# Feed-forward up projections with the weight tiles stationary and the transposed tokens moving

## The reference

```
def squared_relu_mlp(x, w_up, w_down):          # first block, hidden width 4096
    return jnp.square(jax.nn.relu(x @ w_up)) @ w_down

def swiglu(h, w_in, w_out):                     # second block, twice, hidden width 2816
    a, b = jnp.split(h @ w_in, 2, axis=-1)
    return (jax.nn.silu(a) * b) @ w_out
```

## Time and profile before

| | us |
|---|---|
| median of 3 runs | 1234.88 (1234.44, 1234.88, 1235.19) |
| span of the profiled execution, first to last instruction | 1232.4 |
| PE busy | 1114.9 (90%) |
| PE weight loads | 922.5 (75%) |
| DVE busy | 843.9 (68%) |
| ACT busy | 502.0 (41%) |
| stage M, up(0) to the start of its last down | about 152 to 337 |
| stage F2A | about 595 to 787 |
| stage F2B | about 1036 to 1220 |

### The profile page before, as it was taken

How to read it: one execution, slowest core, us unless ns; L and a number is a source line. 1 busy time by engine, 2 the same in 40 slices (tenths; PEclk the granted TensorE clock), 3 DMA queues, 4 the chain that set the end, 5 groups by cost and what they waited for, 6 DMA issues and landing times.

```text
span 1232.4 us, 15193 instructions
## 1 busy us (share of the span) xinstructions
PE 1114.9 (90%) x5509; PEld 922.5 (75%) x5509; DVE 843.9 (68%) x1145; ACT 502.0 (41%) x679; POOL 77.4 (6%) x79
## 2 busy tenths in 40 slices
PE   4999699999969988769999999789969998999997
PEld 3887578888758877767788888589756776788885
DVE  5777566677567778986587778688666876445543
ACT  6335354544434754312434343234244433343441
POOL 1000100000010005530000000000200000000000
PEclk9999899999989999979899999879879999999999
DMA  9961459678367750013398798657212002665541
GB/s 321 353 230 63 154 218 325 241 259 293 128 243 259 276 180 1 1 69 103 134 330 286 283 318 272 221 199 222 69 69 69 2 12 91 205 204 189 169 152 68
DMA packets 125604, 224.28 MB, mean 182 GB/s; under 512 B 4760, under 2 KB 58232, under 8 KB 125432
## 3 DMA queue, kind: packets, MB, share of 16 engines
q1 hardware_dynamic: 124904, 221.02, 51.6%
q0 software_dynamic: 656, 2.69, 0.7%
HBM read 222.64 MB, written 1.05 MB: 182 GB/s over the span
## 4 chain that ended last, share of the span: by engine, by line
PE 49%; DVE 4%; ACT 1%; issue 1%; POOL 0%; POOLq 0%; ACTq 0%; DVEq 0%
PE psum L1365 46%; PE psum L1799 1%; PE psum L1655 1%; DVE arena L927 1%; DVE res L964 0%; DVE arena L963 0%; PE psum L1394 0%; PE psum L1382 0%; DVE xlo L934 0%; ACT arena L822 0%; POOL arena L506 0%; ACT arena L581 0%; DVE arena L913 0%; PE psum L1734 0%; ACT arena L842 0%
## 5 line engine op out<-in xcount | busy, mean ns | idle before, releaser
L872 DVE TENSOR_TENSOR wlo<-raw,whi 128x2048 fp32r<-128x2048 f32 (+2 forms) x172 | 340.3, 1992 | 207.1 <-ACT whi L576 206.8
L576 ACT CAST whi<-raw 128x2048 fp32r<-128x2048 f32 (+2 forms) x172 | 287.2, 1675 | 218.6 <-PE psum L1365 215.8
L1365 PE MATMUL psum<-whi,xhi 128*128 128x512 f32 (+1 forms) x896 | 355.0, 396 | 18.1 <-DVE xlo L934 10.9
L1365 PE MATMUL psum<-whi,xlo 128*128 128x512 f32 (+1 forms) x896 | 350.2, 391 | 0.0
L1365 PE MATMUL psum<-wlo,xhi 128*128 128x512 f32 (+1 forms) x896 | 350.0, 391 | 0.0
L1365 PEld LDWEIGHTS psum<-whi,xhi 128*128 128x128 f32 x896 | 171.7, 192 | 53.5 <-issue 21.5
L1365 PEld LDWEIGHTS psum<-whi,xlo 128*128 128x128 f32 x896 | 171.1, 191 | 34.1
L1365 PEld LDWEIGHTS psum<-wlo,xhi 128*128 128x128 f32 x896 | 171.8, 192 | 32.2
L890 DVE SCALAR_TENSOR_TENSOR adaacc<-adaw,cact,adaacc 128x512 f32<-128x512 f32 x196 | 147.3, 751 | 6.4
L1365 PE MATMUL psum<-whi,hhi 128*128 128x512 f32 x304 | 120.2, 395 | 5.6 <-DVE hlo L1151 2.8
L1365 PE MATMUL psum<-wlo,hhi 128*128 128x512 f32 x304 | 119.0, 391 | 0.0
(11 more groups left out here) (227 smaller groups left out, 1091.3 us busy)
## 6 DMA issues: line engine op xcount, KB each, us to landing
adaw<-in_ada_w SPq DMA_DIRECT2D x48, 1024.0 KB, 5.7
raw<-in_ffn_w_in SPq DMA_DIRECT2D x88, 512.0 KB
raw<-in_ffn_w_out SPq DMA_DIRECT2D x44, 512.0 KB
raw<-in_w_up SPq DMA_DIRECT2D x16, 1024.0 KB
raw<-in_w_down SPq DMA_DIRECT2D x16, 1024.0 KB
raw<-in_hgrn_w_in SPq DMA_DIRECT2D x16, 1024.0 KB
raw<-in_attn_w_qkv SPq DMA_DIRECT2D x12, 1024.0 KB
adaw<-in_kv_ada_w SPq DMA_DIRECT2D x8, 1024.0 KB, 5.2
```

The costliest lines, as they stand in the source:

```text
L576: sc.copy(whi[:, s, 0:width], raw[:, s, 0:width]).then_inc(hi_ready[s], 1)
L872: ve.tensor_tensor(wlo[:, s, 0:width], raw[:, s, 0:width], whi[:, s, 0:width].bitcast(F32), ALU.subtract).then_inc(lo_ready[s], 1)
L1365: return te.matmul(dst, lhsT, rhs, start=start, stop=stop, skip_group_check=open_)
```

## The change

In `up` the roles of the operands are exchanged. The stationary operand is a 128x128 tile of the weights, the moving one all 256 tokens of a depth tile. Four hidden tiles `f` stand in the place of the two token tiles; two of them share a bank. The result comes out with the hidden dimension on the partitions, and the transposes and the semaphore `h_turned` go. In M, ACT's relu now works on 2x256 values of a bank, and its square reads `relu` in SBUF instead of the transposed PSUM. In F2A and F2B one silu over bank 4 and one product with bank 5 replace two of each, and the cast and subtraction read `gat` in SBUF. New waits: PE waits for `act_done` (M) or `gate_done` (F2A, F2B) ahead of the next `up`, ACT for `used[3]` (the down before) ahead of the cast into `hhi`, and ACT (M) and DVE (F2A, F2B) for `h_lo` ahead of writing `sq` and `gat`.

```
             def up(n, fresh=None):
...
-                    for i in range(TT):
+                    for f in range(4):
+                        dst = psum[:, 4 + f // 2, (f % 2) * T:(f % 2 + 1) * T]
                         for k in range(4):
-                            kt = 4 * s + k
-                            ins = three(psum[:, 4 + i, :], xhi[:, kt, i * P:(i + 1) * P], xlo[:, kt, i * P:(i + 1) * P],
-                                        s, k * 512, 512, kt == 0, kt == KD - 1)
+                            kt, c = 4 * s + k, k * 512 + f * P
+                            mm(dst, whi[:, s, c:c + P], xhi[:, kt, :], kt == 0 and f % 2 == 0, False, True)
+                            mm(dst, whi[:, s, c:c + P], xlo[:, kt, :], False, False, True)
+                            ins = mm(dst, wlo[:, s, c:c + P], xhi[:, kt, :], False, kt == KD - 1, True)
                     ins.then_inc(used[s], 1)
...
             up(Q_FF1, fresh=1)
-            hidden1(0)
             with pe.Fori(1, N_FF1) as t:
+                pe.wait_ge(act_done, 2 * t)
                 up(t + Q_FF1)
                 pe.wait_ge(h_lo, 2 * t)
                 down(t + (Q_FF1 - 1), 2, slots=(2,))
+                pe.wait_ge(ada_saved, t + (A_FF1 - 1))
                 ada(t + (A_FF1 - 1))
                 down(t + (Q_FF1 - 1), 2, slots=(3,))
-                hidden1(t)
...
                 up(q0, fresh)
-                mlp2_hidden(0, gb)
                 with pe.Fori(1, N_FF2) as t:
+                    pe.wait_ge(gate_done, t + gb)
                     up(t + q0)
                     pe.wait_ge(h_lo, t + hb)
                     down(t + (q0 - 1), 1)
...
-                    mlp2_hidden(t, gb)
```

ACT in M, ACT in F2A and F2B, and DVE in F2A and F2B:

```
-                for i in range(TT):
-                    sc.activation(relu[:, i, :], psum[:, 4 + i, :], ACT.Relu).then_inc(act_done, 1)
+                for b in range(2):
+                    sc.activation(relu[:, 2 * b:2 * b + 2, :], psum[:, 4 + b, :].rearrange("p (k t) -> p k t", k=2),
+                                  ACT.Relu).then_inc(act_done, 1)
...
                 for b in range(2):
-                    act.wait_ge(h_turned, 2 * t + b + 1)
-                    sc.activation(sq[:, 2 * b:2 * b + 2, :], psum[:, 6 + b, :].rearrange("p (k t) -> p k t", k=2),
-                                  ACT.Square).then_inc(h_sq, 1)
+                    act.wait_ge(act_done, 2 * t + b + 1)
+                    if not first:
+                        act.wait_ge(h_lo, 2 * t)
+                    sc.activation(sq[:, 2 * b:2 * b + 2, :], relu[:, 2 * b:2 * b + 2, :], ACT.Square).then_inc(h_sq, 1)
                     act.wait_ge(h_sq, 2 * t + b + 1)
+                    if not first:
+                        act.wait_ge(used[3], t + Q_FF1)
                     sc.copy(hhi[:, 2 * b:2 * b + 2, :], sq[:, 2 * b:2 * b + 2, :]).then_inc(h_hi, 1)
...
-                for i in range(TT):
-                    sc.activation(sil[:, i, :], psum[:, 4 + i, 0:256], ACT.Silu).then_inc(act_done, 1)
+                sc.activation(sil, psum[:, 4, :].rearrange("p (k t) -> p k t", k=2), ACT.Silu).then_inc(act_done, 1)
...
-                act.wait_ge(h_turned, t + (hb + 1))
-                sc.copy(hhi[:, 0:2, :], psum[:, 6, :].rearrange("p (k t) -> p k t", k=2)).then_inc(h_hi, 1)
+                act.wait_ge(gate_done, t + (gb + 1))
+                if not first:
+                    act.wait_ge(used[3], t + q0)
+                sc.copy(hhi[:, 0:2, :], gat).then_inc(h_hi, 1)
...
-                for i in range(TT):
-                    v.wait_ge(act_done, 2 * t + (gb + 16 + i + 1))
-                    ve.tensor_tensor(gat[:, i, :], sil[:, i, :], psum[:, 4 + i, 256:512], ALU.mult).then_inc(gate_done, 1)
+                v.wait_ge(act_done, t + (gb + 2 * N_FF1 + 1))
+                if not first:
+                    v.wait_ge(h_lo, t + hb)
+                ve.tensor_tensor(gat, sil, psum[:, 5, :].rearrange("p (k t) -> p k t", k=2), ALU.mult).then_inc(gate_done, 1)
...
-                ve.tensor_tensor(hlo[:, 0:2, :], psum[:, 6, :].rearrange("p (k t) -> p k t", k=2),
-                                 hhi[:, 0:2, :].bitcast(F32), ALU.subtract).then_inc(h_lo, 1)
+                ve.tensor_tensor(hlo[:, 0:2, :], gat, hhi[:, 0:2, :].bitcast(F32), ALU.subtract).then_inc(h_lo, 1)
```

More of the change, by code:

```diff
@@ L215, in build @@
         st1 = area(11520, 2, 8)
-        relu = area(0, TT, 512)
+        relu = area(0, 4, T)
         sq = area(1024, 4, T)
-        sil = area(2048, TT, T)
-        gat = area(2560, TT, T)
+        sil = area(2048, 2, T)
+        gat = area(2560, 2, T)
         hin = area(0, 4, TT, D)
@@ L286, in build @@
         acc_done = sem("acc_done")
-        act_done, gate_done, h_turned, h_sq, h_hi, h_lo = [sem(s) for s in ("act_done", "gate_done", "h_turned", "h_sq", "h_hi", "h_lo")]
+        act_done, gate_done, h_sq, h_hi, h_lo = [sem(s) for s in ("act_done", "gate_done", "h_sq", "h_hi", "h_lo")]
         bg_turned, bg_saved = sem("bg_turned"), sem("bg_saved")
@@ L763, in _, with mlp2 @@
             split(3, Q_F2A, 1024)
-            def mlp2(t, q0, hb, first=False, nxt=2048, last=False):
+            def mlp2(t, q0, hb, gb, first=False, nxt=2048, last=False):
                 if not last:
@@ L774, in mlp2 @@
                     split(2, t + q0, 1024)
-                act.wait_ge(h_turned, t + (hb + 1))
-                sc.copy(hhi[:, 0:2, :], psum[:, 6, :].rearrange("p (k t) -> p k t", k=2)).then_inc(h_hi, 1)
+                act.wait_ge(gate_done, t + (gb + 1))
+                if not first:
+                    act.wait_ge(used[3], t + q0)
+                sc.copy(hhi[:, 0:2, :], gat).then_inc(h_hi, 1)
                 if not first:
                     split(3, t + q0, 1024)
-            mlp2(0, Q_F2A, HT_F2A, first=True)
+            mlp2(0, Q_F2A, HT_F2A, 0, first=True)
             with act.Fori(1, N_FF2 - 1) as t:
-                mlp2(t, Q_F2A, HT_F2A)
-            mlp2(N_FF2 - 1, Q_F2A, HT_F2A, nxt=1536)
+                mlp2(t, Q_F2A, HT_F2A, 0)
+            mlp2(N_FF2 - 1, Q_F2A, HT_F2A, 0, nxt=1536)
             split(2, Q_KV, 1536)
@@ L857, in _ @@
             split(3, Q_F2B, 1024)
-            mlp2(0, Q_F2B, HT_F2B, first=True)
+            mlp2(0, Q_F2B, HT_F2B, N_FF2, first=True)
             with act.Fori(1, N_FF2 - 1) as t:
-                mlp2(t, Q_F2B, HT_F2B)
-            mlp2(N_FF2 - 1, Q_F2B, HT_F2B, last=True)
+                mlp2(t, Q_F2B, HT_F2B, N_FF2)
+            mlp2(N_FF2 - 1, Q_F2B, HT_F2B, N_FF2, last=True)
         @block.vector
@@ L1352, in _ @@
             split(3, Q_F2B, 1024)
-            mlp2(0, Q_F2B, HT_F2B, 2 * N_FF2, first=True)
+            mlp2(0, Q_F2B, HT_F2B, N_FF2, first=True)
             with v.Fori(1, N_FF2 - 1) as t:
-                mlp2(t, Q_F2B, HT_F2B, 2 * N_FF2)
-            mlp2(N_FF2 - 1, Q_F2B, HT_F2B, 2 * N_FF2, last=True)
+                mlp2(t, Q_F2B, HT_F2B, N_FF2)
+            mlp2(N_FF2 - 1, Q_F2B, HT_F2B, N_FF2, last=True)
             residual(5)
@@ L1648, in _ @@
             norm(3, gates=2)
[L1650 to L1656, removed]
             def mlp2(q0, hb, gb, fresh, m0=None):
@@ L1818, in _ @@
             norm(5, gates=4)
-            mlp2(Q_F2B, HT_F2B, 2 * N_FF2, 6)
+            mlp2(Q_F2B, HT_F2B, N_FF2, 6)
 _INS = ["x", "norm_mix_pre", "norm_mix_post", "norm_ffn_pre", "norm_ffn_post", "w_up", "w_down", "attn_w_qkv", "attn_w_o",
```

## The result

The changed kernel takes 1236.98 us (median of 15 runs, 1235.82 to 1238.62) where the kernel before takes 1234.85 us (15 runs, 1232.38 to 1235.53) on the same chip. The ratio is 1.0023, 95% interval 1.0015 to 1.0030: 2 to 4 us slower, at the edge of the 2.5 us that I had called no change. I forecast 1235.3 with a range of 1215 to 1251, and 0.39, 0.38 and 0.23 for same, slower and faster.

What follows compares the result with a forecast made beforehand. PE's matmul stream was taken to bound the kernel. Narrow matmuls added 18.4 us and removed transposes, restarts and waits saved about 18.3, so +0.4 with a remaining restart: 1235.3 us, range 1215 to 1251.

Steps and rivals of the forecast that it cites:

- The price of a matmul by its width: In `up`, a matmul of 256 columns costs 0.1200 us, columns plus surcharge; over 30 items this adds 18.4 us.
- 0.1249: Rival pitch in `up`, us a matmul: load and surcharge one after the other, 1249.4 us; chance 0.27 for anything above 0.1209.
- 0.1134: Rival pitch in `up`, us a matmul: the surcharge halves as at 128 columns, 1216.3 us; chance 0.17 for anything below 0.1191.
- 0.1118: Lowest pitch in `up` by the trace, us a matmul: the load's floor, 1211.7 us; within the 0.17 for below 0.1191.
- 0.109: Pitch in `up` by the Trainium skill's back-to-back rule, us a matmul: about 1204 us; chance 0.02 of the 0.17.
- Transposes and restart: PE time removed per item: 0.87 us in M (7 items, -6.1), 0.46 in F2B (ten items, -4.6) and in F2A.
- The wait at the side product in F2A: PE's wait of 0.21 us for DVE ahead of the side product's matmuls disappears, in 9 items.
- The ends: Ahead of the last `down`: M saves 1.05 us (wait 2.75), F2B 0.45 (1.55 instead of 2.00), F2A counted as nothing.
- F2B as a whole: Stage F2B: narrow matmuls added, then -4.6 for transposes and restart, +0.15 at the first item, -0.45 at the end.
- The clock: Side rival: stretches of half clock, 1.75 us for one after F2A's last wait, vanish or appear, -2 to +4 us; chance 0.10.
- The sum: Whole kernel: all terms give +0.05 us, +0.4 with the restart behind F2A's side product, so the saving is paid back.
- From the span to the time: Whole kernel: runs lie 2.5 us above the profiled span, so a span of 1232.8 becomes a time of 1235.3 us.

Runs made afterwards that it cites:

- M only: Exchange of operands and missing transposes in the first feed-forward layer (M) only, F2A and F2B as in the kernel before: 1234.06 us against 1234.24, ratio 1.0000.
- few transposes: The kernel before with 1 of every 4 transposes kept, matmuls and waits otherwise as before: 1223.50 us against 1234.24, ratio 0.9920.
- F2A and F2B only: The change in F2A and F2B only, M as in the kernel before: 1236.36 us against 1234.24, ratio 1.0020.
- the early start: M's last `down` starts slot 2 after the first half of the hidden values: changed kernel 1233.36 us, M only 1230.17, kernel before 1234.74.

## Why the prediction was right, and where it was off

- *The price of a matmul by its width:* right. 0.1200 was taken, 0.1199 measured; the other pitches that I weighed (0.1249, 0.1134, 0.1118, 0.109) fell. The term it carries, +18.4 us for 30 items, stands: 30 x (11.51-10.91) = 18.0.
- *Transposes and restart:* right. By the periods, an item of M gained 0.25 (0.26 forecast), one of F2A 0.05 (0.06), one of F2B lost 0.19 (0.15, taken from a period 0.03 longer than the others).
- *The wait at the side product in F2A:* right, it went.
- *The ends:* M's last `down` starts 3.06 us after the start of the matmul ahead, 2.83 after the stream, where I had 2.75; the one of F2B 1.65 after the stream, where I had 1.55. Small shortfalls. At F2A's end, where I took nothing, the last `down` starts 8.08 us after the one before it, instead of 8.28.
- *F2B as a whole:* was to lose 1.8 (6.7-4.6+0.15-0.45) and lost 2.26. Most of the difference is the period, nine times 0.04 us, and the rest the end. I also left the restart behind the first wait out of the new order, though PE's first two matmuls there are 0.2 apart as after any wait. That is about 0.1 us, but it doesn't show in the sum: the stretch from F2B's start to its first `down` grew by 0.86 us (25.44 to 26.30), where my terms give 0.9.
- *The clock:* it made most of the distance between forecast and result. I had priced a stretch of half clock at 1.75 us and named F2A's end for it; it kept its place there. In the profiled execution a new one came at M's last `down`, 1.62 us, and M's start had 0.94 us more of it, while F2A's start had about 0.6 less than before. I had given the clock as a side rival, with -2 to +4 us, and not in the sum.
- *The sum:* +0.4 forecast, +2 to +4 measured. Of the profiled execution's 3.9 us, the three stages make +0.8, M's last `down` 1.6, the stretches between 0.9 and the one ahead of M 0.65. At equal clocks the three stages come to -2.1 (M, as in M only), about +0.3 (F2A) and +2.3 (F2B), together about +0.5, against -2.2, +0.7 and +1.8 by my terms. So the even trade is what the mechanism gives. That the misses in F2A and F2B cancel is luck, and so is that the clock, which the sum left out, took no more than it did.
- *From the span to the time:* harmless, since the forecast is the median plus 0.4. But not all of the 2.5 us lies around the span: every run that lists both has its time 1.8 above its span. The profiled execution before was thus one of about 1234.2, a little faster than the median.

## What to carry to other kernels

To exchange stationary and moving operands is paid in loads: count the matmuls before and after, and price them at columns/2.4 GHz plus the surcharge measured beside them, never below the load's own time. Here an item pays 0.61 us against 0.87 (8 transposes) or 0.46 (4), so the exchange can be worth it only in the stage with 8, and there its 2.1 us didn't reach the kernel's time by themselves. Where a product depends on halves of a buffer, try to wait for the half: with the exchange in M that edit gave the only kernels that beat the one before, though alone it gave nothing that the runs could show.

## What the runs showed of the hardware that was not expected

- At full clock a matmul costs more than its moving columns, by 13 to 14 ns with 128 columns loaded (streams of 256, 384 and 512 columns) and by 7 ns with 64 (256). At half clock, 256 columns with 128 loaded cost nothing beyond the columns.
- In stretches hundreds of microseconds long that an edit did not touch, the granted clock differed between kernels by 0.01 to 0.02, worth about 1 us. Where PE waits a few microseconds, the half clock may follow or not in kernels that are alike there: at M's end in the changed kernel, in M only and with few transposes; not in the kernel before, with F2A and F2B only, nor with the early start.
- Whether the edits did this is not shown. Each kernel has one trace, and executions of one kernel differ as much: the mean granted clock of the changed kernel's 15 runs lies between 0.939 and 0.946.
